# Three of the norm's scales and shifts as TensorE's sums, 36 matmuls ahead of them, the row of c loaded behind x

## The chip, the cores and the metric

One core of one Trainium2 chip runs the whole program in one launch. The time is device microseconds of that core, the median of several runs; lower is better. TensorE (PE) does matmuls, VectorE (DVE) and ScalarE (ACT) the elementwise work; SyncE (SP) issues nearly all DMAs from one queue, in the order of its program.

## The reference, cut to what matters

The program is two blocks over x of 512 tokens by 1024 features. The first begins with an adaptive norm, whose scale and shift come from a row c:

```python
mod = jax.nn.silu(c) @ w_ada[layer] + b_ada[layer]
shift1, scale1, gate1, shift2, scale2, gate2 = [m[:, None, :] for m in jnp.split(mod, N_MOD, axis=-1)]
h = rms_norm(x, g_pre_mix[layer]) * (1.0 + scale1) + shift1
proj = h @ w_in[layer]          # [512, 1024] @ [1024, 3584]
```

Behind it come a convolution and a retention mixer, an MLP of 4096, a pooling mixer and a recurrent mixer with 16 heads, each between large projections. All is float32.

## The kernel before, in words

**The data.** Weights come in units of 128 partitions by 1024 float32 (512 KB). `unit_list()` (line 32) gives their order: matmul units (True) and units of w_ada (False). SyncE loads them in this order (`load`, line 403), each into a slot: a ring of 5 slots of RAW, and six units (5 to 10) into free rows of Z. A unit loaded into a used slot first waits for what emptied it, and everything behind it in the queue waits too. The order at the start is, with u for one unit: w_in 0, ada 0, ada 1, w_in 1, ada 2, ada 3, ada 4, ada 5, w_in 2, ada 6, ada 7, ada 8, ada 9, w_in 3, ada 10 to ada 15, w_in 4 and so on. These are units 0 to 19; unit 18 (ada 14) takes the slot of unit 13 (w_in 3) and unit 19 (ada 15) that of unit 14 (ada 10).

**A matmul unit** is split into a high part (WH, ScalarE, line 1671) and a low part (WL, VectorE, line 967), both in the fp32r format; the normed tokens are split likewise into HH and HL. Each product is three matmuls (`three`, lines 488 to 490): high by high, high by low, low by high.

**The norm's scale and shift.** For f from 0 to 7, ada 2f holds the weights of the scale of features 128f to 128f+127, one feature on each partition, and ada 2f+1 those of their shift. `first_modulation` (line 931) multiplies a unit by CB, which is silu(c) on every partition (line 1142), and sums along the row, on VectorE (line 937). ScalarE adds the biases (lines 1861 and 1865), applies scale and shift to the transposed tokens (line 1871) and rounds to HH (line 1874); VectorE makes HL (`first_low`, line 1155). VectorE's order for each f is: ada 2f, ada 2f+1, HL of f-1, and at f = 1, 3, 5 the low part of the next w_in unit.

**TensorE** transposes the normed tokens (`first_tokens`, line 631; the instruction's inputs are float32), and runs `group`, the first projection: for k from 0 to 7, 12 matmuls of 512 columns once HL of k is there. The column products that follow have all they need as soon as HH and HL are whole.

**Ahead of that** SyncE issues: vectors, constants, the row of c broadcast to 128 partitions (line 413), four tiles of x (line 415), the units. VectorE and ScalarE make silu(c) as columns (COL) and as rows (CB), the squares of x (lines 1145, 1757), the root (lines 1035 to 1053) and the normed tokens (lines 1067 and 1761). ScalarE's line 1847 is the sigmoid of the row of c.

All orders are written out by hand, an instruction stream for each engine; the waits are on counts of semaphores. `taken` counts units that VectorE has finished with, `banks.made` tells that TensorE has filled a PSUM bank.

Of the kernel before, what the change touches and what calls it, by code (L numbers as in the profile page):

```python
# [10 lines left out]
ALU = mybir.AluOpType  # L11
# [20 lines left out]
def unit_list():  # L32

    out = []
    for f in range(8):
        if f in (0, 1, 3, 5):
            out.append(("w_in", (f + 1) // 2, True))
        out += [("ada", 2 * f, False), ("ada", 2 * f + 1, False)]
    ada = iter(range(16, 48))  # L40
    for n in range(4, 28):
        out.append(("w_in", n, True))
        if n >= 12:
            out += [("ada", next(ada), False) for _ in range(1 + n % 2)]
    for name, n in (("w_out", 8), ("w_fc1", 32), ("w_fc2", 32), ("pool_in", 40), ("pool_out", 16),
                    ("hgrn_in", 64), ("hgrn_out", 16)):
        for i in range(n):
            out.append((name, i, True))
            if name == "w_fc1" and 6 <= i < 14:
                out.append(("ada", next(ada), False))  # L50
    return out

UNITS = unit_list()
GEMM = [i for i, u in enumerate(UNITS) if u[2]]
LENGTH = {name: sum(u[0] == name and u[2] for u in UNITS) for name in dict.fromkeys(u[0] for u in UNITS)}

# [152 lines left out]
def build(nc, a):  # L210
    with ExitStack() as ctx:
# [64 lines left out]
        def flat(i):  # L276

            return Z[:, i:i + 2, :].rearrange("p a b -> p (a b)")
# [122 lines left out]
        def sync_program(e):  # L401
            def load(i):
                name, n, _ = UNITS[i]
                if RBEFORE[i] is not None:
                    e.wait_ge(taken.sem, taken.of(RBEFORE[i]))
                e.dma_start(raw(i), a[name][n]).then_inc(s_raw[RSLOT[i]], 16)

            def row(to, i):
                e.dma_start(to, a["rows"][i].partition_broadcast(128)).then_inc(s_row, 16)

            e.dma_start(VEC[:, :], a["vec"]).then_inc(s_vec, 16)
            e.dma_start(CST[:, :], a["cst"][:, 0:C_D]).then_inc(s_cst, 16)
            e.dma_start(flat(0), a["rows"][5].partition_broadcast(128)).then_inc(s_c, 16)
            for t in range(4):
                e.dma_start(X[:, t, :], a["x"][128 * t:128 * t + 128, :]).then_inc(s_x[t], 16)
            for i in range(20):
                load(i)
            e.dma_start(POSI, a["positions"].partition_broadcast(128)).then_inc(s_pos, 16)
            for i in range(20, 25):
                load(i)  # L420
            e.dma_start(MSK[:, :], a["msk"]).then_inc(s_msk, 16)
            e.dma_start(DMASK, a["cst"][:, C_D:C_N]).then_inc(s_d, 16)
            for i in range(25, len(UNITS)):
                load(i)

                if UNITS[i][0:2] == ("w_in", 10):
                    e.wait_ge(hlo.sem, hlo.of("in", 7))
                    row(flat(24), 0)
                    row(flat(2), 1)
                if UNITS[i][0:2] == ("w_fc1", 12):  # L430
                    e.wait_ge(tdone.sem, tdone.of("out", "x", 3))
                    row(flat(28), 2)
                    row(flat(30), 3)
                if UNITS[i][0:2] == ("pool_in", 12):
                    e.wait_ge(*banks.taken(("fc2", 3, 1)))
                    row(G[:, :], 4)
            for t in range(3):
                e.wait_ge(zdone.sem, zdone.of("final", t))
                e.dma_start(a["out"][128 * t:128 * t + 128, :], flat(2 * t)).then_inc(s_out, 16)
            for n in range(2):  # L440
                if n == 0:
                    e.wait_ge(zdone.sem, zdone.of("final", 3))
                else:
                    e.wait_ge(normed.sem, normed.of("final"))
                e.dma_start(a["out"][384:512, 512 * n:512 * n + 512], flat(6)[:, 512 * n:512 * n + 512]).then_inc(
                    s_out, 16)
            e.wait_ge(s_out, 16 * 5)

        def tensor_program(e):  # L450
# [176 lines left out]
            def first_tokens(f):  # L627
# [4 lines left out]
                                    IDN)  # L632
                m.then_inc(banks.full[b], banks.fill(("x", "t", f), b))

            e.wait_ge(own.sem, own.of("ones"))
            e.wait_ge(s_cst, 16)
            e.wait_ge(normed.sem, normed.of("x", 1))
            e.wait_ge(own.sem, own.of("normed", "x", 3))
            for f in range(4):
                first_tokens(f)  # L640
            for k, _ in enumerate(group([("v", j) for j in range(4)], [0, 1, 2, 3], True, "in")):
                if k < 4:
                    first_tokens(4 + k)
# [260 lines left out]
        def vector_program(e):  # L904
# [26 lines left out]
            def first_modulation(f):  # L931

                for j in (1, 0):
                    i = UNITS.index(("ada", 2 * f + 1 - j, False))
                    e.wait_ge(*landed(i))
                    c = 8 if j else 16
                    e.scalar_tensor_tensor(out=raw(i), in0=raw(i), scalar=1.0, in1=CB[:, :], op0=ALU.mult, op1=ALU.mult,  # L937
                                           accum_out=MOD[:, c + f:c + f + 1]).then_inc(taken.sem, taken(i))
# [169 lines left out]
            def boundary(stage, gain):  # L1108
# [13 lines left out]
                if stage != "pout":  # L1122
# [10 lines left out]
            e.memset(ONES[:, :], 1.0).then_inc(own.sem, own("ones"))  # L1133
            e.wait_ge(s_vec, 16)
            e.wait_ge(copied.sem, copied.of("silu"))
            e.tensor_tensor(COL[:, 0:8], COL[:, 8:16], VEC[:, V_C:V_C + 8], ALU.mult).then_inc(own.sem, own())
            e.scalar_tensor_tensor(out=GB, in0=VEC[:, V_BADA + 8:V_BADA + 16], scalar=1.0,
                                   in1=VEC[:, V_GPRE1:V_GPRE1 + 8], op0=ALU.add, op1=ALU.mult).then_inc(
                                       own.sem, own("gb"))
            e.wait_ge(s_c, 16)  # L1140
            e.wait_ge(copied.sem, copied.of("silu row"))
            e.tensor_tensor(CB[:, :], flat(2), flat(0), ALU.mult).then_inc(own.sem, own("cb"))
            for t in (1, 3):
                e.wait_ge(s_x[t], 16)
                e.scalar_tensor_tensor(out=flat(2 + 2 * t), in0=X[:, t, :], scalar=1.0 / 1024, in1=X[:, t, :],
# [3 lines left out]
            token_factors("x", 0, 4)  # L1149
            normed_tokens("x", 2)  # L1150
            normed_tokens("x", 3)

            def first_low(k):
                e.wait_ge(hhi.sem, hhi.of("in", k))
# [2 lines left out]

            p.next, p.hi, p.unit = 20, 4, 4
            lo_to(1)
            for f in range(8):  # L1160
                first_modulation(f)
                if f:
                    first_low(f - 1)
                if f in (1, 3, 5):
                    lo_to((f + 3) // 2)
# [492 lines left out]
        def scalar_program(e):  # L1658
# [101 lines left out]
            def normed_tokens(stage, t):  # L1760
                e.activation(normal(stage, t), X[:, t, :], ACT.Copy, scale=RT[:, t:t + 1]).then_inc(
                    normed.sem, normed(stage, t))
# [80 lines left out]

            e.wait_ge(s_vec, 16)
            e.activation(COL[:, 8:16], VEC[:, V_C:V_C + 8], ACT.Sigmoid).then_inc(copied.sem, copied("silu"))
            e.wait_ge(s_c, 16)
            e.activation(flat(2), flat(0), ACT.Sigmoid).then_inc(copied.sem, copied("silu row"))
            for t in (0, 2):
                e.wait_ge(s_x[t], 16)
                token_squares("x", t)  # L1850
            hi_to(1)
            e.wait_ge(own.sem, own.of("factors", "x", 0))
            normed_tokens("x", 0)
            normed_tokens("x", 1)
            e.wait_ge(own.sem, own.of("gb"))
            for f in range(8):
                b = 4 + f % 4
                if f in (1, 3, 5):
                    hi_to((f + 3) // 2)
                e.wait_ge(taken.sem, taken.of(UNITS.index(("ada", 2 * f, False))))  # L1860
                e.activation(GA[:, f:f + 1], MOD[:, 8 + f:9 + f], ACT.Identity,
                             scale=VEC[:, V_GPRE1 + f:V_GPRE1 + f + 1], bias=GB[:, f:f + 1]).then_inc(
                                 copied.sem, copied())
                e.wait_ge(taken.sem, taken.of(UNITS.index(("ada", 2 * f + 1, False))))
                e.activation(MOD[:, f:f + 1], MOD[:, 16 + f:17 + f], ACT.Identity,
                             bias=VEC[:, V_BADA + f:V_BADA + f + 1]).then_inc(copied.sem, copied())
                if f > 1:
                    e.wait_ge(hlo.sem, hlo.of("in", f - 2))
                e.wait_ge(*banks.made(("x", "t", f)))
                e.wait_ge(copied.sem, copied.n)  # L1870
                e.activation(TMP[:, 2 + f % 2, :], PS[b][:, :], ACT.Identity, scale=GA[:, f:f + 1],
                             bias=MOD[:, f:f + 1]).then_inc(banks.free[b], 1)
                e.wait_ge(*banks.taken(("x", "t", f)))
                e.activation(HH[:, f, :], TMP[:, 2 + f % 2, :], ACT.Copy).then_inc(hhi.sem, hhi("in", f))
# [425 lines left out]
```

## Time and profile before

| | us |
|---|---|
| median of 3 runs | 1482.09 (1479.09 to 1482.83) |
| the profiled execution | 1482.02 |
| its span | 1480.2 |
| PE busy in the span | 1445.2 (98%) |
| DVE busy | 871.0 (59%) |
| ACT busy | 563.5 (38%) |

The span is what the trace covers, from the first to the last instruction; 1.8 us of the execution's time lie outside it. PE's busy time is of pipelined matmuls with modelled ends, so the distance from one start to the next says more than the length of one. Every window of the trace begins at the span's start.

### The profile page before, as it was taken

Reading aid. Unit: us, or ns where it says so; the run is one execution under the profiler, and the core shown is the slowest. Engines: PE = TensorE matmul, PEld = TensorE weight load, DVE = VectorE, ACT = ScalarE, POOL = GpSimd, SP = SyncE. Lnnn points to the kernel's source line nnn. Section 1 sums busy time; section 2 is a strip of 40 time slices with the busy share of each in tenths; the row PEclk is TensorE's granted clock in tenths of the full one; section 3 lists DMA queues with packets and bytes.
Section 4 is the critical chain, followed back from the end, with each engine's and each line's share of the span. In section 5 each row is a group of like instructions: output and inputs, shape, how many; then the busy total and the mean of one; then the engine's idle time right before and its main releaser. Section 6 shows DMA issues by size and latency. Waiting matters only on the chain.

```text
span 1480.2 us, 18490 instructions
## 1 busy us (share of the span) xinstructions
PE 1445.2 (98%) x7204; PEld 1202.9 (81%) x7204; DVE 871.0 (59%) x1718; ACT 563.5 (38%) x1025; POOL 0.2 (0%) x4
## 2 busy tenths in 40 slices
PE   4999999999999999999999999999999999999998
PEld 3788788988888887988888888888888888888786
DVE  7876767543333335656457435325878777788545
ACT  5422345422232224533333334333444444444331
POOL 0000000000000000000000000000000000000000
PEclk9999999999999999999999999999999999999999
DMA  8645542353233334123233232232222222122221
GB/s 330 219 142 213 185 157 72 127 199 96 90 100 100 98 91 139 51 92 115 73 98 121 81 112 89 96 100 72 72 62 67 72 72 67 63 72 72 71 71 58
DMA packets 43863, 158.31 MB, mean 107 GB/s; under 512 B 4864, under 2 KB 5248, under 8 KB 43776
## 3 DMA queue, kind: packets, MB, share of 16 engines
q1 hardware_dynamic: 43776, 157.12, 32.4%
q8 instruction: 58, 0.95, 0.3%
q14 instruction: 29, 0.24, 0.1%
HBM read 155.00 MB, written 2.10 MB: 106 GB/s over the span
## 4 chain that ended last, share of the span: by engine, by line
PE 93%; DVE 4%; DMA 1%; ACT 1%; issue 1%; SPq 0%; ACTq 0%; DVEq 0%
PE PS L488 29%; PE PS L490 28%; PE PS L489 28%; PE PS L772 1%; PE PS L820 1%; PE PS L783 1%; PE PS L484 1%; PE PS L824 1%; PE PS L814 1%; PE PS L792 1%; PE PS L800 1%; DVE RAW L937 1%; DMA X<-in_x 1%; PE PS L839 1%; DVE WL L967 0%
## 5 line engine op out<-in xcount | busy, mean ns | idle before, releaser
L488 PE MATMUL PS<-HH,WH 128*128 128x512 f32 (+1 forms) x1088 | 432.2, 397 | 0.0
L490 PE MATMUL PS<-HH,WL 128*128 128x512 f32 (+1 forms) x1088 | 418.3, 384 | 0.0
L489 PE MATMUL PS<-HL,WH 128*128 128x512 f32 (+1 forms) x1088 | 417.2, 383 | 0.0
L967 DVE TENSOR_TENSOR WL<-RAW,WH 128x1024 fp32r<-128x1024 f32 x219 | 266.3, 1220 | 73.4 <-ACT WH L1671 73.1
L1671 ACT ACTIVATE WH<-RAW 128x1024 fp32r<-128x1024 f32 x219 | 230.8, 1057 | 185.5 <-PE PS L490 145.9
L490 PEld LDWEIGHTS PS<-HH,WL 128*128 128x128 f32 x1088 | 204.4, 188 | 42.0
L488 PEld LDWEIGHTS PS<-HH,WH 128*128 128x128 f32 x1088 | 204.8, 188 | 37.6 <-issue 1.0
L489 PEld LDWEIGHTS PS<-HL,WH 128*128 128x128 f32 x1088 | 205.0, 188 | 37.0 <-issue 1.0
L488 PE MATMUL PS<-WH,ZH 128*128 128x512 f32 x400 | 155.9, 390 | 0.0
L490 PE MATMUL PS<-WH,ZL 128*128 128x512 f32 x400 | 155.6, 389 | 0.0
L489 PE MATMUL PS<-WL,ZH 128*128 128x512 f32 x400 | 155.6, 389 | 0.0
L1014 DVE TENSOR_TENSOR ZL<-Z,ZH 128x512 fp32r<-128x512 f32 x52 | 35.6, 691 | 141.8 <-ACT ZH L1730 141.8
L1730 ACT ACTIVATE ZH<-Z 128x512 fp32r<-128x512 f32 x52 | 32.4, 632 | 156.9 <-PE PS L490 156.9
L488 PE MATMUL PS<-WH,HH 128*128 128x512 f32 x208 | 84.2, 405 | 4.8 <-DVE HL L1155 4.8
L489 PEld LDWEIGHTS PS<-WL,ZH 128*128 128x128 f32 x400 | 75.1, 188 | 15.6
L490 PEld LDWEIGHTS PS<-WH,ZL 128*128 128x128 f32 x400 | 75.1, 188 | 15.6
L488 PEld LDWEIGHTS PS<-WH,ZH 128*128 128x128 f32 x400 | 75.1, 188 | 15.4
L490 PE MATMUL PS<-WH,HL 128*128 128x512 f32 x208 | 82.4, 396 | 0.0
L489 PE MATMUL PS<-WL,HH 128*128 128x512 f32 x208 | 82.2, 395 | 0.0
L1316 DVE TENSOR_TENSOR Z<-TMP 128x512 f32<-128x512 f32 x32 | 22.0, 693 | 90.4 <-ACT TMP L1965 90.3
L1965 ACT ACTIVATE TMP<-PS 128x512 f32<-128x512 f32 x32 | 19.0, 598 | 109.9 <-PE PS L490 109.6
L488 PEld LDWEIGHTS PS<-WH,HH 128*128 128x128 f32 x208 | 39.9, 192 | 14.2 <-DVE RAW L937 2.9
(259 smaller groups left out, 1774.2 us busy)
## 6 DMA issues: line engine op xcount, KB each, us to landing
RAW<-in_w_fc SPq DMA_DIRECT2D x64, 512.0 KB, 3.5
RAW<-in_hgrn_in SPq DMA_DIRECT2D x64, 512.0 KB, 3.5
RAW<-in_ada SPq DMA_DIRECT2D x43, 512.0 KB, 4.6
RAW<-in_pool_in SPq DMA_DIRECT2D x40, 512.0 KB, 3.6
RAW<-in_w_in SPq DMA_DIRECT2D x27, 512.0 KB, 4.5
RAW<-in_pool_out SPq DMA_DIRECT2D x16, 512.0 KB, 3.6
RAW<-in_hgrn_out SPq DMA_DIRECT2D x16, 512.0 KB, 3.5
RAW<-in_w_out SPq DMA_DIRECT2D x8, 512.0 KB, 4.1
```

Of the source, the lines that this page charges most:

```text
L484: m = e.transpose(PS[b][:, c:c + 128], normal(stage, t)[:, 128 * f:128 * f + 128], IDN)
L488: e.matmul(out, wh, xh, start=first, stop=False)
L489: e.matmul(out, wh, xl, start=False, stop=False)
L490: return e.matmul(out, wl, xh, start=False, stop=last)
L772: m = e.matmul(PAIR[:, 256 * i:256 * i + 192], t.f[:, c], t.qp[:, i, :], start=True, stop=True)
L783: m = e.matmul(PS[b][:, 64 * i:64 * i + 64].rearrange("p (n l) -> p n l", l=16), t.k[:, c], halves(t.q[:, c], 16)[1], start=True, stop=True)
L967: e.tensor_tensor(lo, raw(i), hi.bitcast(F32), ALU.subtract).then_inc(taken.sem, taken(i))
L1014: e.tensor_tensor(lo, Z[:, k, :], hi.bitcast(F32), ALU.subtract).then_inc(zlo.sem, zlo(z))
L1316: e.tensor_tensor(Z[:, f, :], TMP[:, f % 2, :], TMP[:, f % 2, :], ALU.mult).then_inc(zdone.sem, zdone("fc1", f))
L1671: e.activation(place(s)[0], raw(i), ACT.Copy).then_inc(whi.sem, whi(s))
L1730: e.activation(z_place(z)[0], Z[:, k, :], ACT.Copy).then_inc(zhi.sem, zhi(z))
L1965: e.activation(TMP[:, f % 2, :], PS[b][:, :], ACT.Relu).then_inc(banks.free[b], 1)
```

## The change

The order of the units changes at the start (w_in 0 and w_in 1 behind the ada units of their f). Three ada units (0, 1 and 3: scale and shift of f = 0, shift of f = 1) are laid out by the host with the contraction on the partitions, and `first_sums` makes their sums on TensorE, eight matmuls of one column for each, with COL as the moving operand. Bank 0 holds those of f = 0, bank 1 that of f = 1; ScalarE reads them in PSUM. TensorE begins with 36 matmuls of ONES by ONES (float32, 128 columns), whose result nothing reads. The row of c is loaded behind the four tiles of x, its sigmoid comes behind ScalarE's squares, and CB behind VectorE's normed tokens. The high part of w_in 0 comes behind ScalarE's normed tokens.

```diff
     for f in range(8):
-        if f in (0, 1, 3, 5):
+        if f in (3, 5):
             out.append(("w_in", (f + 1) // 2, True))
         out += [("ada", 2 * f, False), ("ada", 2 * f + 1, False)]
+        if f < 2:
+            out.append(("w_in", f, True))
...
+SUMMED = {0: 0, 1: 0, 3: 1}
...
             def load(i):
                 name, n, _ = UNITS[i]
                 if RBEFORE[i] is not None:
-                    e.wait_ge(taken.sem, taken.of(RBEFORE[i]))
+                    was = UNITS[RBEFORE[i]]
+                    if was[0] == "ada" and was[1] in SUMMED:
+                        e.wait_ge(*banks.made(("mod", SUMMED[was[1]])))
+                    else:
+                        e.wait_ge(taken.sem, taken.of(RBEFORE[i]))
...
-            e.dma_start(flat(0), a["rows"][5].partition_broadcast(128)).then_inc(s_c, 16)
             for t in range(4):
                 e.dma_start(X[:, t, :], a["x"][128 * t:128 * t + 128, :]).then_inc(s_x[t], 16)
+            e.dma_start(flat(0), a["rows"][5].partition_broadcast(128)).then_inc(s_c, 16)
...
+            def first_sums(b):
+                claim(b)
+                n = [u for u in SUMMED if SUMMED[u] == b]
+                for c, u in enumerate(n):
+                    i = UNITS.index(("ada", u, False))
+                    e.wait_ge(*landed(i))
+                    for k in range(8):
+                        m = e.matmul(PS[b][:, c:c + 1], raw(i)[:, 128 * k:128 * k + 128], COL[:, k:k + 1],
+                                     start=k == 0, stop=k == 7)
+                m.then_inc(banks.full[b], banks.fill(("mod", b), b))
             e.wait_ge(own.sem, own.of("ones"))
+            for _ in range(36):
+                e.matmul(PS[2][:, 0:128], ONES[:, :], ONES[:, :], start=True, stop=True)
+            e.wait_ge(own.sem, own.of("silu"))
+            first_sums(0)
             e.wait_ge(s_cst, 16)
             e.wait_ge(normed.sem, normed.of("x", 1))
             e.wait_ge(own.sem, own.of("normed", "x", 3))
             for f in range(4):
                 first_tokens(f)
+            first_sums(1)
...
             def first_modulation(f):
                 for j in (1, 0):
+                    if 2 * f + 1 - j in SUMMED:
+                        continue
...
             e.scalar_tensor_tensor(out=GB, ...)
-            e.wait_ge(s_c, 16)
-            e.wait_ge(copied.sem, copied.of("silu row"))
-            e.tensor_tensor(CB[:, :], flat(2), flat(0), ALU.mult).then_inc(own.sem, own("cb"))
...
             normed_tokens("x", 3)
+            e.wait_ge(s_c, 16)
+            e.wait_ge(copied.sem, copied.of("silu row"))
+            e.tensor_tensor(CB[:, :], flat(2), flat(0), ALU.mult).then_inc(own.sem, own("cb"))
...
-            e.wait_ge(s_c, 16)
-            e.activation(flat(2), flat(0), ACT.Sigmoid).then_inc(copied.sem, copied("silu row"))
             for t in (0, 2):
                 e.wait_ge(s_x[t], 16)
                 token_squares("x", t)
-            hi_to(1)
+            e.wait_ge(s_c, 16)
+            e.activation(flat(2), flat(0), ACT.Sigmoid).then_inc(copied.sem, copied("silu row"))
             e.wait_ge(own.sem, own.of("factors", "x", 0))
             normed_tokens("x", 0)
             normed_tokens("x", 1)
+            hi_to(1)
...
-                e.wait_ge(taken.sem, taken.of(UNITS.index(("ada", 2 * f, False))))
-                e.activation(GA[:, f:f + 1], MOD[:, 8 + f:9 + f], ACT.Identity,
+                if f == 0:
+                    e.wait_ge(*banks.made(("mod", 0)))
+                else:
+                    e.wait_ge(taken.sem, taken.of(UNITS.index(("ada", 2 * f, False))))
+                e.activation(GA[:, f:f + 1], PS[0][:, 0:1] if f == 0 else MOD[:, 8 + f:9 + f], ACT.Identity,
...
+                shift = (PS[0][:, 1:2], PS[1][:, 0:1])[f] if f < 2 else MOD[:, 16 + f:17 + f]
+                if f < 2:
+                    e.wait_ge(*banks.made(("mod", f)))
+                else:
+                    e.wait_ge(taken.sem, taken.of(UNITS.index(("ada", 2 * f + 1, False))))
+                m = e.activation(MOD[:, f:f + 1], shift, ACT.Identity, bias=VEC[:, V_BADA + f:V_BADA + f + 1])
```

## Rows read from the trace of the kernel before

**Rows 1.** Busy time by window: stretch, length, engines, PEclk, DMA share, GB/s.
```profile
0.00:60.00 60.00, 37.30 (x155) 30.20 (x156) 44.61 (x79) 34.77 (x56) 0.20 (x4) 0.97 0.81 297
60.00:1480.00 1420.00, 1407.91 (x7050) 1172.65 (x7048) 826.37 (x1640) 528.68 (x970) 0.00 (x0) 1.00 0.31 99
```

**Rows 2.** The chain that ended last, 30 to 48 us: start, length, what.
```profile
37.11 1.14 DVE WL L967
...
38.65 6.08 DMA RAW<-in_ada
...
45.98 0.61 DVE HL L1155
```

**Rows 3.** Timeline of DVE: start, length, line, operation, count, idle before.
```profile
8.19 1.23 DVE L1142 TENSOR_TENSOR CB<-Z 128x1024 f32<-128x1024 f32 x1 [4.98 <-ACT Z L1847]
...
12.45 1.23 DVE L1145 SCALAR_TENSOR_TENSOR Z<-X 128x1024 f32<-128x1024 f32 x1 [1.43 <-DMA X<-in_x]
...
15.50 1.42 DVE L1067 TENSOR_SCALAR Z<-X,COL 128x1024 f32<-128x1024 f32 x2
16.83 1.22 DVE L967 TENSOR_TENSOR WL<-RAW,WH 128x1024 fp32r<-128x1024 f32 x1
17.96 1.22 DVE L937 SCALAR_TENSOR_TENSOR RAW<-RAW,CB 128x1024 f32<-128x1024 f32 x1
...
19.11 1.22 DVE L937 SCALAR_TENSOR_TENSOR RAW<-RAW,CB 128x1024 f32<-128x1024 f32 x1
...
26.61 0.69 DVE L1155 TENSOR_TENSOR HL<-TMP,HH 128x512 fp32r<-128x512 f32 x1
27.21 1.22 DVE L937 SCALAR_TENSOR_TENSOR Z<-Z,CB 128x1024 f32<-128x1024 f32 x1
...
44.75 1.23 DVE L937 SCALAR_TENSOR_TENSOR RAW<-RAW,CB 128x1024 f32<-128x1024 f32 x1 [1.12 <-DMA RAW<-in_ada]
```

**Rows 4.** Timeline of ACT.
```profile
13.73 1.06 ACT L1671 ACTIVATE WH<-RAW 128x1024 fp32r<-128x1024 f32 x1 [1.42 <-DMA RAW<-in_w_in]
15.50 2.19 ACT L1761 ACTIVATE Z<-X,COL 128x1024 f32<-128x1024 f32 x2 [0.71 <-DVE COL L1053]
...
20.37 0.29 ACT L1865 ACTIVATE MOD<-MOD,VEC 128x1 f32<-128x1 f32 x1 [0.70 <-DVE RAW L937]
20.76 0.78 ACT L1871 ACTIVATE TMP<-PS,MOD,COL 128x512 f32<-128x512 f32 x1
21.57 0.63 ACT L1874 ACTIVATE HH<-TMP 128x512 fp32r<-128x512 f32 x1
22.10 1.04 ACT L1671 ACTIVATE WH<-RAW 128x1024 fp32r<-128x1024 f32 x1
```

**Rows 5.** Timeline of PE, matmuls alone, 17 to 60 us.
```profile
17.94 3.65 PE L631 MATMUL PS<-CST,Z 128*128 128x128 f32 x16 [17.94 <-ACT Z L1761]
23.38 0.76 PE L488 MATMUL PS<-WH,HH 128*128 128x512 f32 x1 [1.79 <-DVE HL L1155]
...
26.85 0.40 PE L490 MATMUL PS<-WH,HL 128*128 128x512 f32 x1
...
27.78 0.60 PE L631 MATMUL PS<-CST,Z 128*128 128x128 f32 x4
28.14 0.48 PE L488 MATMUL PS<-WH,HH 128*128 128x512 f32 x1
...
46.73 0.47 PE L488 MATMUL PS<-WH,HH 128*128 128x512 f32 x1 [2.52 <-DVE HL L1155]
...
50.68 0.40 PE L489 MATMUL PS<-WL,HH 128*128 128x512 f32 x1
```

**Rows 6.** Timeline of PE, 119.8 to 121 us, float32 matmuls of the retention.
```profile
119.85 1.05 PE L660 MATMUL PS<-Z 128*128 128x128 f32 x8
120.66 0.48 PE L488 MATMUL PS<-HH,WH 128*128 128x512 f32 x1
```

**Rows 7.** Busy time by window, one that has DMA throughout.
```profile
24.00:27.00 3.00, 3.00 (x9) 2.38 (x8) 3.00 (x6) 1.77 (x4) 0.00 (x0) 1.00 1.02 407
```

More of the change, by code:

```diff
@@ L1135, in vector_program @@
             e.wait_ge(copied.sem, copied.of("silu"))
-            e.tensor_tensor(COL[:, 0:8], COL[:, 8:16], VEC[:, V_C:V_C + 8], ALU.mult).then_inc(own.sem, own())
+            e.tensor_tensor(COL[:, 0:8], COL[:, 8:16], VEC[:, V_C:V_C + 8], ALU.mult).then_inc(
+                own.sem, own("silu"))
             e.scalar_tensor_tensor(out=GB, in0=VEC[:, V_BADA + 8:V_BADA + 16], scalar=1.0,
@@ L1159, in vector_program @@
             lo_to(1)
+            e.wait_ge(own.sem, own.of("cb"))
             for f in range(8):
@@ L1859, in scalar_program @@
                     hi_to((f + 3) // 2)
-                e.wait_ge(taken.sem, taken.of(UNITS.index(("ada", 2 * f, False))))
-                e.activation(GA[:, f:f + 1], MOD[:, 8 + f:9 + f], ACT.Identity,
+                if f == 0:
[3 more added lines that the diff above has]
+                e.activation(GA[:, f:f + 1], PS[0][:, 0:1] if f == 0 else MOD[:, 8 + f:9 + f], ACT.Identity,
                              scale=VEC[:, V_GPRE1 + f:V_GPRE1 + f + 1], bias=GB[:, f:f + 1]).then_inc(
                                  copied.sem, copied())
-                e.wait_ge(taken.sem, taken.of(UNITS.index(("ada", 2 * f + 1, False))))
-                e.activation(MOD[:, f:f + 1], MOD[:, 16 + f:17 + f], ACT.Identity,
-                             bias=VEC[:, V_BADA + f:V_BADA + f + 1]).then_inc(copied.sem, copied())
+                shift = (PS[0][:, 1:2], PS[1][:, 0:1])[f] if f < 2 else MOD[:, 16 + f:17 + f]
[4 more added lines that the diff above has]
+                m = e.activation(MOD[:, f:f + 1], shift, ACT.Identity, bias=VEC[:, V_BADA + f:V_BADA + f + 1])
+                if f < 2:
+                    m.then_inc(banks.free[f], 1)
+                    e.wait_ge(*banks.taken(("mod", f)))
+                else:
+                    m.then_inc(copied.sem, copied())
                 if f > 1:
@@ L2266 @@
     features = ada.T.reshape(48, 128, 1024)
+    scale_shift = features[[8 * j + f for f in range(8) for j in (1, 0)]]
+    sums = columns(ada)[[8 * j + f for f in range(8) for j in (1, 0)]]
     arrays = {
@@ L2278 @@
         "msk": msk,
-        "ada": np.concatenate([features[[8 * j + f for f in range(8) for j in (1, 0)]], shares[16:24],
+        "ada": np.concatenate([np.stack([(sums if u in SUMMED else scale_shift)[u] for u in range(16)]), shares[16:24],
                                features[24:40], shares[40:48]]),
```

## The prediction

> **What bounds the kernel now.** I read the windows first. From 60 us to the end TensorE is busy for 1407.91 of 1420 us; before 60 us only for 37.30 of 60 [rows 1]. All edits lie in the first 45 us, so they can shift the start of TensorE's long stretch and little else. What is worth asking is when that stretch begins, and who sets it.
>
> The chain from 30 to 48 us answers [rows 2]. VectorE makes the low part of w_in 3, which ends at 38.25. That frees the slot for ada 14, and ada 15 is queued behind it; the DMA on the chain starts at 38.65 and lasts 6.08 us; VectorE sums ada 15 from 44.75 [rows 3]; HL of k = 6 starts at 45.98; TensorE takes k = 6 up at 46.73 after 2.52 us idle [rows 5]. Behind it nothing waits in this stage. So the end moves with the moment at which VectorE finishes w_in 3 (call it L3, 38.25), if the rest of the chain keeps its 8.48 us.
>
> TensorE's records also show two speeds: 0.43 us for 512 columns (1.2 GHz) from 23.38 to 26.85 and from about 47.3 to 50.68, 0.23 us (2.4 GHz) between and behind [rows 5]. The first slow stretch costs nothing, as the stage waits for VectorE anyway. The second costs some eight matmuls by 0.20 us = 1.6 us, and it followed the idle 2.52 us.
>
> **VectorE's side, taken away.** Three sums leave, at 1.15 us each by the distance of two starts, 17.96 and 19.11 [rows 3]: 3.45 us. CB (1.23) does not leave; it stood at 8.19, in time in which VectorE waited for x, and comes behind the normed tokens, where VectorE is busy: +1.2. The row of c goes behind x: it is 512 KB, at 407 GB/s [rows 7] 1.28 us, so the last tile of x is there 1.28 earlier and its squares start at 11.15 instead of 12.45; the root then ends 3.05 later at 14.2 (15.50 before) [rows 3]. Normed tokens (1.42 for two [rows 3]) to 15.6, CB to 16.8. The row itself lands at about 12.4, its sigmoid is done by 13.5, so CB waits for neither.
>
> The low part of w_in 0 needs its high part. ScalarE now makes its normed tokens first: 14.2 + 2.19 = 16.4, and the high part follows, 1.06, to 17.4 [rows 4]. The unit is third in the queue now: w_in 0 landed at 13.73 as the first [rows 4], the third place lands at 16.3. VectorE starts the low part at 17.45, against 16.83: 0.6 late. The saving of 1.28 is used up by CB and by this step. Low part to 18.6, ada 2 to 19.75 (landed 17.5).
>
> **TensorE's side, added.** The 36 matmuls of ONES write a bank that is not in use, from about 1.0. Nothing in the trace is such a matmul. The retention's float32 products are nearest: 8 records from 119.85 to 120.66 [rows 6], that are four matmuls, since each float32 product has two records: 0.20 us a matmul at 2.4 GHz. The slow end: transposes, with one record each, take 3.65/16 = 0.22 at the start and 0.09 (27.78 to 28.14 for four) later [rows 5]; two records at the slow pace are 0.43. Ends: 36 x 0.20 = 7.2 and 36 x 0.43 = 15.5. I take slow for some 4 us, as in both slow stretches, then fast: 9 x 0.43 + 27 x 0.20 = 9.3, to 10.4. TensorE is then idle until ada 0 lands (first place, 13.7), 3.3 us, more than the 2.52 that put it back. So I take the sums as beginning slow: 8 x 0.43 = 3.4 to 17.1, then 8 x 0.20 to 18.7. Bank 0 is seen at 18.9. The 16 transposes at 0.09 go to 20.2; ada 3 has landed at 18.8; eight more sums to 21.8. A sum of one column has no row either; below its price is that of a fast transpose (0.09), above it the slow 0.43; weight loads are as wide as in the retention, so I keep 0.20 fast.
>
> The Trainium skill bears on two of these choices. "TensorE: Matmul & The Clock Gate", HAM oscillation, says that waiting between bursts puts the clock back, and that each burst starts cold again; the trace agrees at 46.73, and by this rule the 36 matmuls buy nothing for the sums, as I have it. The same page, LDWEIGHTS, makes a weight load of 128 columns 128/1.2 = 107 ns at any clock; by that the sums would be 0.21 each even slow (an estimate), bank 0 would be full at 17.3, and the total would be that of the first rival.
>
> **ScalarE and the chain of k = 0 and 1.** Scale 0 from 19.0, shift 0, the application from 19.75, HH from 20.55 [rows 4], the high part of w_in 1 from 21.1 (22.10 - 21.57 behind HH). Shift 1 comes at 22.35, with bank 1 seen at 22.0; then 0.39 to the application (20.37 to 20.76), 0.81 to HH, 0.63 for it: 24.2. On VectorE, HL 0 ends at 21.8, the low part of w_in 1 waits to 22.2 and ends at 23.35, ada 4 and 5 at 25.65 (landed 21.4 and 22.7), HL 1 at 26.25 (0.60 as from 26.61 to 27.21 [rows 3]). HH 1 is not waited for, by 1.5 us.
>
> **From there to L3** the order is as before: six sums (ada 6 to 11) 6.9, three HL 1.8, two low parts 2.27, together 11.0. ada 6 and 7 land at 25.2 and 26.5 by 1.28 each, and ada 11 at 32.9; none is late in this line. L3 = 26.25 + 11.0 = 37.25. That is 1.0 us earlier than 38.25. Of 3.45 us taken away, 2.45 are lost to the later start, to HH 0, which now hangs on bank 0, and to w_in 1 behind it.
>
> **Waits added.** SyncE waits for bank 0 (18.9, before: 18.05) with units 11 to 15 behind it, and for bank 1 with unit 15. By the 1.28 us a unit, unit 11 has its place in the stream at 27.8 and unit 15 at 32.9; they go out 8.9 and 10.9 us ahead of that, more than the 6.08 of the DMA on the chain [rows 2], so the stream has no gap. ScalarE waits for bank 0 with everything behind it; that is in the sum. The host's new layout costs nothing on the device.
>
> **Sum.** The profiled execution has 1482.0; less 1.0 it is 1481.0. It stands 0.07 below the median of 1482.09, so the time is 1481.0. By my line TensorE waits before k = 6 as long as now, so the second slow stretch stays. What a measurement can't tell from no change is 0.3%, 4.4 us.
>
> **Rivals.**
> 1. The clock holds, or the sums cost 0.20 at any clock: bank 0 at 17.2, bank 1 at 20.2. Then ScalarE is early and only landings bound VectorE: ada 7 at 26.5, and from there ada 7 to 11, three HL and two low parts, 5 x 1.15 + 3 x 0.60 + 2 x 1.14 = 9.8; L3 = 36.3, 1.9 earlier: 1480.1. For it: float32 products are real matmuls, not transposes. Against: 3.3 us idle.
> 2. As the forecast or the first rival, and the wait before k = 6 falls so that the clock stays up: 1.6 more, 1478.5 to 1479.4. For it: TensorE may end k = 5 later than I think, and a shorter idle stretch may not put it back. Against: 2.52 us did, and nothing shortens the DMA in the chain.
> 3. Slower: TensorE at 1.2 GHz stands in the norm's path. ScalarE cannot apply f = 1 before bank 1, and HL 1 ends 2.6 us behind bank 1; VectorE is in order. Break-even is HL 1 at 38.25 - 11.0 = 27.25, bank 1 at 24.7. If the slow clock lasts from 13.7 through both rounds: 16 x 0.43 = 6.9 to 20.6, transposes 3.5 to 24.1, 3.4 to 27.5, HL 1 at 30.1, L3 at 41.1, +2.9: 1484.9. If even the 36 run slow, they end at 16.5, all is 2.8 later, +5.7: 1487.7. For it: the transposes at the start ran slow throughout [rows 5]. Against: both slow stretches ended after some 4 us.
> 4. No effect: ada 15's landing doesn't move with L3, as other DMAs fill the time: 1482.0. Against: the chain has the DMA issued right behind L3.
>
> **How the numbers follow.** Forecast 0.42, first rival 0.20, second 0.10, third 0.15 (a third of it in the upper case), fourth 0.13. The executions before spread by 3.7 us, so each case carries some 1.5 us to either side. The range is 1477.0 (second rival, less the spread) to 1485.5 (third rival's first case). Faster by over 0.3% needs below 1477.7: 0.07, second rival with the spread. Slower by over 0.3% needs above 1486.5: 0.06. Within: 0.87.
>
> **What would show it.** VectorE's low part of w_in 0 at 17.4, not 16.8; L3 at 37.2; ada 15 summed from 43.7; k = 6 at 45.7 with a slow stretch behind it; eight of the first 16 sums slow. Wrong if bank 1 is full after 24.7, if the 36 matmuls end after 13.7, if VectorE waits for a landing between ada 6 and w_in 3, or if TensorE from 60 us on is less busy than 1407.91 of 1420.

## The result, and the profile after

| | kernel before | changed kernel |
|---|---|---|
| median | 1481.63 us (1479.09 to 1483.60, 20 runs) | 1478.53 us (1476.67 to 1480.54, 20 runs) |
| ratio | | 0.9981, 95% interval 0.9974 to 0.9988 |
| the profiled execution, and its span | 1482.02, 1480.2 | 1478.98, 1476.9 |

The changed kernel is 2.8 us (by the ratio) to 3.1 us (by the medians) faster. Forecast were 1.0 us and 1481.0. The sign and the range hold, the size is short by two thirds.

By window, TensorE's time (stretch, length, PE, PEld, DVE, ACT, POOL, PEclk, DMA share, GB/s) in the changed kernel:

```profile
0.00:60.00 60.00, 57.31 (x290) 50.70 (x291) 43.03 (x75) 36.13 (x57) 0.20 (x4) 0.89 0.84 305
60.00:1476.00 1416.00, 1404.70 (x7036) 1169.94 (x7034) 824.58 (x1638) 527.16 (x968) 0.00 (x0) 1.00 0.30 99
```

Behind 60 us TensorE is idle for 11.3 us, nearly as before (12.1 [rows 1]). All that changed lies in the first 60 us. The change added 20 us of busy time there, nearly all of it dummy matmuls and sums; busy time is no measure of gain. What counts is the start of the first column product, as TensorE hardly waits behind it. From there to the end of the span it is 1426.3 us in both profiles.

Timeline of PE in the changed kernel: start, length, line (658: ONES; 651: the sums; 639: transposes; 496 to 498: `three`), operands, count, idle before:

```profile
1.04 10.62 PE L658 MATMUL PS<-ONES 128*128 128x128 f32 x72 [1.04 <-DVE ONES L1161]
13.31 4.37 PE L651 MATMUL PS<-COL,RAW 128*128 128x1 f32 x32 [1.65 <-DVE COL L1081]
17.54 3.65 PE L639 MATMUL PS<-CST,Z 128*128 128x128 f32 x16
20.99 3.41 PE L651 MATMUL PS<-COL,RAW 128*128 128x1 f32 x16
24.26 0.77 PE L496 MATMUL PS<-WH,HH 128*128 128x512 f32 x1
...
30.03 0.47 PE L496 MATMUL PS<-WH,HH 128*128 128x512 f32 x1
...
45.20 0.39 PE L496 MATMUL PS<-WH,HH 128*128 128x512 f32 x1
...
50.64 0.39 PE L496 MATMUL PS<-HH,WH 128*128 128x512 f32 x1
```

The value group starts at 24.26 (23.38 before [rows 5]), later and not earlier, and the column products at 50.64. In the trace of before that row stands at 53.89, which is 3.25 later. The 72 records of ONES are the 36 matmuls. After 13.31 no row has idle time in front of it, k = 6 (45.20) included; before, TensorE idled 2.52 us there [rows 5]. So in this profile it is no longer VectorE but TensorE's own stream that sets the end. The chain that ended last runs over TensorE alone from 13.31 on (start, length, what):

```profile
13.31 4.37 PE PS L651 x32
17.68 3.52 PE PS L639 x16
21.20 3.21 PE PS L651 x16
24.40 0.64 PE PS L496
```

Granted clock of the changed kernel (stretch, length, PE, PEclk, DMA share, GB/s):

```profile
14.00:16.00 2.00, 2.00 (x21) 1.00 1.03 422
16.00:18.00 2.00, 2.00 (x12) 0.54 1.04 420
24.00:26.00 2.00, 2.00 (x6) 0.50 1.03 410
28.00:30.00 2.00, 2.00 (x9) 0.55 1.03 410
```

It falls to half, 1.2 GHz, soon after 16 and comes back only at the end of k = 0, close to 30. There is no second slow stretch. This column can read 1.00 where the pace of the records says 1.2 GHz: in the kernel before it reads 1.00 from 24 to 27 us [rows 7], where the rows stand 0.43 us apart [rows 5].

Timeline of DVE in the changed kernel (965: sums, 995: low parts, 1184: HL):

```profile
26.20 0.69 DVE L1184 TENSOR_TENSOR HL<-TMP,HH 128x512 fp32r<-128x512 f32 x1 [1.55 <-ACT HH L1915]
...
36.63 1.22 DVE L995 TENSOR_TENSOR WL<-RAW,WH 128x1024 fp32r<-128x1024 f32 x1
37.76 1.22 DVE L965 SCALAR_TENSOR_TENSOR RAW<-RAW,CB 128x1024 f32<-128x1024 f32 x1
...
41.40 1.22 DVE L965 SCALAR_TENSOR_TENSOR RAW<-RAW,CB 128x1024 f32<-128x1024 f32 x1 [0.66 <-DMA RAW<-in_ada]
...
42.67 1.22 DVE L965 SCALAR_TENSOR_TENSOR RAW<-RAW,CB 128x1024 f32<-128x1024 f32 x1
```

Count L3 here as the start of the instruction behind the low part of w_in 3: 37.76, and 38.16 in the trace of before. The 3.25 us then split in three. L3 is 0.40 earlier. Ada 15 is summed from 42.67, 4.91 behind L3, where it was 44.75 - 38.16 = 6.59 [rows 3]: 1.68. From that sum to the first column product it is 7.97 against 9.14: 1.17. In the eight profiles below in which TensorE stays fast and VectorE sets k = 6 or nearly so (e1, e3, e5, e6, e8 to e11) this distance is 7.51 to 7.55, so the second slow stretch, which is missing, was worth 1.6, and 0.4 of it is lost as TensorE comes late to k = 6. Only the first part is what the change was said to do; the experiments are about the other two.

### The profile page after: what moved, and what is told of

It is laid out like the page before. It is cut to its first block, busy times and chain, and to the rows that moved or that the text cites. A ratio compares the mean times of both kernels' runs of the same rounds, so it can differ in the third digit from the quotient of the medians.

```text
span 1476.9 us, 18725 instructions
## 1 busy us (share of the span) xinstructions
PE 1462.0 (99%) x7324; PEld 1220.6 (83%) x7324; DVE 867.6 (59%) x1712; ACT 563.3 (38%) x1025; POOL 0.2 (0%) x4
## 4 chain that ended last, share of the span: by engine, by line
PE 95%; DVE 2%; ACT 1%; issue 1%; DMA 0%; SPq 0%; ACTq 0%; DVEq 0%
PE PS L496 29%; PE PS L498 28%; PE PS L497 28%; PE PS L798 1%; PE PS L846 1%; PE PS L809 1%; PE PS L492 1%; PE PS L850 1%; PE PS L840 1%; PE PS L818 1%; PE PS L826 1%; PE PS L865 1%; PE PS L651 1%; DMA X<-in_x 0%; PE PS L639 0%
## 5 line engine op out<-in xcount | busy, mean ns | idle before, releaser
L1503 DVE RECIPROCAL DG<-W 128x96 f32<-128x96 f32 (+1 forms) x64 | 49.7, 821 | 0.0
```

The source lines that it names most:

```text
L1503: e.reciprocal(i8[:, n, l], w8[:, n, l]).then_inc(own.sem, own("iw", h, i))
```

## The experiments

Each kernel was timed in 5 rounds beside the kernel before on the same chip (the last one has a single execution). The table gathers the profiles, one execution of each kernel, which can lie 1.1 us off the kernel's median (e2: 1481.8 and 1480.73, e9: 1478.09 and 1479.24); "packet" is the start of the 16 KB packet of the queue `q8 instruction` that lies nearest to L3.

| kernel | L3 | ada 15 summed, behind L3 | idle before k = 6 | slow stretch at k = 6 | first column product | packet | ratio (95%) |
|---|---|---|---|---|---|---|---|
| before | 38.16 | 6.59 | 2.52 | yes | 53.89 | 38.3 | |
| changed | 37.76 | 4.91 | none | no | 50.64 | 48.1 | 0.9981 (0.9974 to 0.9988) |
| e1_no_warm | 38.61 | 4.99 | 0.93 | no | 51.12 | 31.8 | 0.9992 (0.9983 to 1.0001) |
| e2_bridge | 36.36 | 6.91 | 2.85 | yes | 53.68 | 36.4 | 1.0000 (0.9992 to 1.0009) |
| e3_fill_k6 | 37.31 | 7.30 | 0.69 | no | 52.12 | 37.4 | 1.0002 (0.9993 to 1.0010) |
| e4_row_moved | 37.18 | 6.84 | 2.79 | yes | 53.18 | 37.2 | 1.0001 (0.9993 to 1.0010) |
| e5_positions_later | 37.19 | 6.76 | 2.33 | no | 51.49 | 37.3 | 1.0003 (0.9994 to 1.0011) |
| e6_two_sums | 36.13 | 5.01 | 0.94 | no | 48.67 | 47.7 | 0.9973 (0.9963 to 0.9984) |
| e7_bridge_fill | 38.00 | 7.07 | none | no | 53.75 | 38.0 | 1.0000 (0.9991 to 1.0009) |
| e8_after_again | 36.36 | 5.07 | 1.01 | no | 48.98 | 44.3 | 0.9976 (0.9966 to 0.9986) |
| e9_ones_only | 37.62 | 4.86 | 0.24 | no | 49.99 | 26.5 | 0.9984 (0.9975 to 0.9993) |
| e10_two_sums_order | 36.86 | 4.04 | none | no | 48.44 | 46.3 | 0.9971 (0.9960 to 0.9981) |
| e11_order_only | 37.08 | 4.32 | 0.26 | no | 48.95 | 40.6 | 0.9971 (0.9960 to 0.9982) |
| e12_before_again | 37.34 | 7.24 | 3.18 | yes | 53.74 | 37.5 | |

**e1_no_warm**: the changed kernel without the 36 matmuls.

```diff
-            for _ in range(36):
-                e.matmul(PS[2][:, 0:128], ONES[:, :], ONES[:, :], start=True, stop=True)
```

> The changed kernel without the 36 matmuls of ONES. Theory T (in the changed kernel TensorE itself sets the end of the value group: it starts the group at 24.26 us and is never idle after that): the 16 sums of f = 0 run at the slow pace of the later ones (0.204 us a record and not 0.132), bank 0 is full 2.3 us later, and so is the start of the group; the first column product starts at 52.9 instead of 50.64, the time is 2.3 us above the changed kernel. Rival V (VectorE and the landing of ada 15 set the end, as the prediction had it): VectorE's low part of w_in 3 ends up to 2.3 later, TensorE idles before k = 6, second slow stretch back: 2.3 + 1.6 = 3.9 us later. Rival W (the 36 matmuls buy nothing): no change within 0.5 us.

Measured: 1479.05 against 1480.73. The 32 records of the first sums take 6.96 us and not 4.37, as expected, but the 16 transposes behind them take 3.65 us, as in the changed kernel, and the pace comes back during the last sums (2.20 us for 16 records, not 3.41), so the first column product is hardly later: 51.12, not 52.9. By the ratios, which come from different chips, 1.6 us of the change's 2.8 are lost without the 36. None of the three theories gives this number, but the intervals of the two ratios overlap, so the times alone rule out neither T nor W.

**e2_bridge**: 45 matmuls and not 36.

```diff
-            for _ in range(36):
+            for _ in range(45):
```

> The changed kernel with 45 matmuls of ONES and not 36, so that TensorE has work until ada 0 lands (about 13.3 us) and the idle 1.65 us before the sums are gone. If the idle stretch is what took the clock down at 16.4: the sums, the transposes and the first k run fast, the value group starts at about 20.5 (HL of k = 0), then waits for VectorE at several k; theory T then expects an end bounded by HL of k = 6 at about 44 and k = 6, 7 at 5.5 us fast: first column product at 49.2 to 49.6, 1.0 to 1.4 us less time; with a second slow stretch 50.8, no gain. If it was not the idle stretch but the sums of one column and the transposes, which do not hold the clock: it falls by 20 us all the same, the group starts 0.5 to 2 earlier and still slow, first column product 0 to 1.3 earlier.

Measured: 1480.73, the same as before the change. Nine matmuls more give the whole gain back, which neither expectation has. TensorE's front is faster than in the changed kernel and L3 is early, but ada 15 is 6.91 behind it, TensorE idles before k = 6 and runs slow behind that.

```profile
14.02 3.90 PE L651 MATMUL PS<-COL,RAW 128*128 128x1 f32 x32
...
45.26 0.77 PE L496 MATMUL PS<-WH,HH 128*128 128x512 f32 x1 [2.85 <-DVE HL L1184]
...
53.68 0.39 PE L496 MATMUL PS<-HH,WH 128*128 128x512 f32 x1
```

These are rows of its PE timeline. As to the clock: no idle time stands before the sums, and it falls all the same.

```profile
16.00:18.00 2.00, 2.00 (x16) 0.81 0.99 397
18.00:20.00 2.00, 2.00 (x11) 0.50 1.05 420
20.00:22.00 2.00, 2.00 (x18) 0.84 1.01 404
```

So the fall does not need the idle 1.65 us. It came while sums of one column and transposes ran, but that these are the cause is not shown: the clock also came back while they ran (20 to 22 us here), and in e6 it reads 1.00 until 18 us, through the sums and the first 16 transposes.

**e3_fill_k6**: the kernel before, with matmuls in the idle time.

```diff
+                        if fresh and k == 6:
+                            claim(4)
+                            for _ in range(11):
+                                e.matmul(PS[4][:, 0:128], ONES[:, :], ONES[:, :], start=True, stop=True)
                         if fresh:
                             e.wait_ge(hlo.sem, hlo.of(fresh, k))
```

> The kernel before, and nothing of the change: ahead of the wait for HL of k = 6 TensorE runs 11 matmuls of ONES by ONES (float32, 128 columns) into bank 4, which is free there, about 2.2 us of work in the 2.5 us in which it was idle. If the idle stretch caused the second slow stretch (47.3 to 50.7): that stretch is gone, first column product at 52.3 instead of 53.9, 1.6 us less time. If it did not: the same time as the kernel before, or up to 0.3 more.

Measured: in the profile as expected, first column product at 52.12 and no slow stretch; in the timed runs nothing, 1480.62 against 1480.73. They would agree if the slow stretch were a matter of chance in the kernel before. e5 shows such a case: idle 2.33 and no slow stretch behind it. The mean granted clock of the single executions points the same way: it was 0.999 in the profiles of e3 and e5 and 0.998 in the three with the stretch and no matmul at the start (before, e4, e12). Of the 78 executions of the kernel before that were timed beside the experiments 21 had 0.999 and took 1480.1 us on average, the other 57 took 1481.4; e3 had 0.999 in 7 of 11. That the stretch makes this difference is not shown, as these executions have no profile.

**e4_row_moved**: the moves of the row of c alone, in the kernel before.

```diff
-            e.dma_start(flat(0), a["rows"][5].partition_broadcast(128)).then_inc(s_c, 16)
             for t in range(4):
                 e.dma_start(X[:, t, :], a["x"][128 * t:128 * t + 128, :]).then_inc(s_x[t], 16)
+            e.dma_start(flat(0), a["rows"][5].partition_broadcast(128)).then_inc(s_c, 16)
...
-            e.wait_ge(s_c, 16)
-            e.wait_ge(copied.sem, copied.of("silu row"))
-            e.tensor_tensor(CB[:, :], flat(2), flat(0), ALU.mult).then_inc(own.sem, own("cb"))
...
             normed_tokens("x", 3)
+            e.wait_ge(s_c, 16)
+            e.wait_ge(copied.sem, copied.of("silu row"))
+            e.tensor_tensor(CB[:, :], flat(2), flat(0), ALU.mult).then_inc(own.sem, own("cb"))
```

> The kernel before with the moves alone: the row of c loaded behind x, its sigmoid behind ScalarE's squares, CB behind VectorE's normed tokens, the high part of w_in 0 behind ScalarE's normed tokens; all 16 sums stay on VectorE. Theory T: x's last tile is there 2 us earlier, but the low part of w_in 0 starts only 0.2 to 0.5 earlier (its high part waits for the normed tokens), VectorE then goes on as before: 0 to 0.5 us less time. Rival (the move of the row carries the gain, as it brought x forward by 2.2 us): 2 us less.

Measured: 1481.26 against 1480.73, no difference. The row's move alone buys nothing that can be measured: ahead of the low part of w_in 0 VectorE now has CB (1.22 us) and 0.62 us of waiting for the high part, and ada 15 lands as late as before.

**e5_positions_later**: one DMA moved, in the kernel before.

```diff
-            e.dma_start(POSI, a["positions"].partition_broadcast(128)).then_inc(s_pos, 16)
             for i in range(20, 25):
                 load(i)
+            e.dma_start(POSI, a["positions"].partition_broadcast(128)).then_inc(s_pos, 16)
```

> The kernel before with one DMA moved: the positions, broadcast to 128 partitions, are issued behind unit 24 and not between units 19 and 20. In four of six profiles the last ada unit landed 6.1 to 6.8 us behind L3, in two 4.5 or less, and the GB/s of that stretch fall to 180 to 300 at a full DMA share. Theory P (the small pieces of the positions slow ada 15's DMA when they overlap it): ada 15 lands 4.4 us behind its issue, k = 6 starts at 45 instead of 46.7, 1.5 to 1.7 us less time, and if TensorE's idle stretch shrinks under 1 us the second slow stretch goes too, 3 us less. Rival (w_in units or chance slow it): no change within 0.5 us.

Measured: 1481.34 against 1481.12, and ada 15 is 6.76 behind L3. The positions are not what slows it. (TensorE also idles 0.65 us at 57.7 in this profile, for a low part.)

**e6_two_sums**: the shift of f = 1 back on VectorE.

```diff
-SUMMED = {0: 0, 1: 0, 3: 1}
+SUMMED = {0: 0, 1: 0}
...
-            first_sums(1)
```

> The changed kernel with the sums of f = 0 alone on TensorE; the shift of f = 1 is VectorE's again. TensorE can start the value group at about 21.2 instead of 24.26; VectorE's chain is hardly longer, as it waited 1.55 us for HH of k = 1 in the changed kernel. Theory K (the changed kernel gains because TensorE, late and slow at k = 0, has no idle stretch before k = 6 and so no second slow stretch): TensorE idles 1.5 to 2.8 us before k = 6 again, the first column product starts at 51.7 to 53 and not 50.64, so 1 to 2.4 us more time than the changed kernel. Rival (each sum taken off the critical start is a gain): 0 to 3 us less than the changed kernel.

Measured: 1477.02 against 1481.12, 0.9973, at least as fast as the changed kernel on that chip (0.9976). That is the rival's side, and my theory K falls: TensorE starts its group at 20.58, idles only 0.94 before k = 6, as ada 15 is early, and stays fast. The gain does not need a late, slow TensorE. The third sum buys nothing that these runs can tell.

**e7_bridge_fill**: 45 matmuls, and 14 before k = 6.

> The changed kernel with 45 matmuls of ONES at the start (no idle stretch before the sums) and 14 more ahead of the wait for HL of k = 6, in bank 4. With the 45 alone VectorE's L3 was at 36.45 but TensorE idled 2.85 us before k = 6 and then ran 24 matmuls at the slow pace, and the first column product started at 53.68. Theory K: with the idle stretch filled, k = 6 and 7 run fast: 45.3 + 5.5 = 50.8 with the late landing of ada 15, 49.2 with the early one: 2.9 to 4.5 us less than with the 45 alone, 0 to 1.4 less than the changed kernel. Rival (the clock falls all the same, or the fillers delay k = 6): 53.7, no gain.

Measured: 1481.17 against 1481.12. No idle time, no slow stretch at k = 6 and still 53.75: here bank 1 was full only at 24.6, and ada 15 was late again. TensorE reached k = 6 at 45.13, and the 28 records held it until 48.17. HL of k = 6 began at 46.22, and TensorE follows such a start by 0.83 us (45.90 to 46.73 before), so some 1.1 us of the 14 matmuls were too many: the rival's side. What a fill of the right length brings with the late DMA this run does not show.

**e8_after_again**: the changed kernel.

> The changed kernel again, as a measure of how much one profile says: if its gain is lasting, the first column product starts at 50.6 to 51.5 again with no slow stretch before it and the ratio is 0.998; if the landing of ada 15 or the clock varies from one execution to the next, it starts up to 2 us later in this profile.

Measured: 1477.65 against 1481.12, 0.9976. Ada 15 is 5.07 behind L3 again, on another chip. So the landing belongs to the program. The first column product does not repeat so well: 48.98, where 50.6 to 51.5 was expected, as here the clock came back before the third sum and bank 1 was full at 22.8. With e1 and e6 that is four profiles under 5.1 and, before e9, six over 6.5, with nothing between.

The packet tells them apart. The DMA view's line for each queue (queue, kind: packets, MB, share of 16 engines), first of the kernel before from 38 to 40 us, then of e2_bridge from 36 to 38, then of the changed kernel from 36 to 41:

```profile
q1 hardware_dynamic: 33, 0.14, 38.7%
q8 instruction: 1, 0.02, 3.0%
```

```profile
q1 hardware_dynamic: 20, 0.08, 31.9%
q8 instruction: 1, 0.02, 4.0%
```

```profile
q1 hardware_dynamic: 258, 0.93, 57.2%
```

In the changed kernel no such packet falls into this stretch, in which ada 14 and 15 are issued; the next is at 48.1. In the page of either kernel there are 58 of them:

```profile
q8 instruction: 58, 0.95, 0.3%
```

TensorE has 7204 matmuls and as many weight loads before, 248 to a packet, and with 45 matmuls at the start there are 59 packets. So I take the packets for TensorE's instructions, brought in as it goes along. The Trainium skill, "Runtime: NRT & Kernel Launch", Instruction fetch mechanics, says that an engine's instructions come in blocks of 16 KiB, 256 of them, by a DMA queue that the sequencer drives; the counts here agree. It also calls the cost of such a block mostly hidden. TensorE shows no wait for one here; what it does to the DMAs beside it the page does not say, and the next run tests it.

**e9_ones_only**: the kernel before with the 36 matmuls at the start, nothing else.

```diff
             e.wait_ge(own.sem, own.of("ones"))
+            for _ in range(36):
+                e.matmul(PS[2][:, 0:128], ONES[:, :], ONES[:, :], start=True, stop=True)
```

> The kernel before with the 36 matmuls of ONES at the start of TensorE's program and nothing else. The profiles so far fall into two kinds: where a 16 KB packet of the instruction queue (q8) falls between 36.4 and 38.3 us, just around the issue of ada 14 and 15 (the kernel before, 45 matmuls with and without the fillers, the filler alone, the row alone, the positions alone), ada 15 lands 6 us or more behind its issue; where it falls elsewhere (the changed kernel twice, without the 36, with two sums) 4.9 or less. Theory Q (that packet is TensorE's own instructions, every so many of them, and where it falls sets the landing): the 36 matmuls move it to about 22 us, ada 15 lands 4.4 to 4.9 us behind its issue, L3 stays, the first column product starts about 2 us earlier, up to 3.6 if the second slow stretch goes with the shorter idle time: 2 to 3.6 us less than before. Theory K (clock and sums alone carry the gain): TensorE has nothing to do from 11 to 17 us and the clock falls again: no change.

Measured: 1479.24 against 1481.62, 0.9984 (0.9975 to 0.9993). 36 matmuls whose result nobody reads, ahead of an idle stretch of 5.96 us, bring 2.4 us, where the whole change brings 2.8 and, in e8, 3.6; the intervals overlap, so what the rest of the change adds is not told from nothing. The packet fell into 26 to 28 us (predicted about 22). The chain of this kernel, and below it that of the kernel before on the same chip (start, length, what):

```profile
37.73 3.48 DMA RAW<-in_ada
...
42.48 1.23 DVE RAW L939 x2
43.71 0.61 DVE HL L1157
...
44.46 0.47 PE PS L488
44.93 0.23 PE PS L489
```

```profile
36.28 1.14 DVE WL L967
37.42 0.40 DVE RAW L937
37.81 6.74 DMA RAW<-in_ada
...
44.58 1.23 DVE RAW L937 x2
...
46.56 0.53 PE PS L488
47.09 0.43 PE PS L489
```

L3 is at 37.62 and 37.34. The chain runs over ada 14 in the one, 3.48 us, as ada 15 is already there when VectorE comes to it, and over ada 15 in the other, 6.74 us. TensorE's clock at the start cannot be the cause: with the 36 it was at half when the group started (0.50 from 22 to 28 us), and the gain came all the same. The clock has its part behind the landing: with 0.24 us idle before k = 6 there is no slow stretch (7.51 from ada 15's sum to the first column product, 9.16 in e12).

Part of the delay stands in SyncE's own rows, the issues of ada 14 and 15 (start, length; first e9, then e12):

```profile
37.73 0.80 SPq L406 DMA_DIRECT2D RAW<-in_ada  x2
```

```profile
37.44 1.41 SPq L406 DMA_DIRECT2D RAW<-in_ada  x2
```

Taken alone, the issue of ada 15 takes 0.43 us in all five profiles in which it lands early and 0.83 to 1.34 in all seven in which it lands late. So 0.4 to 0.9 of the some 2 us pass while SyncE issues the load, beside the packet, and the rest passes behind that.

**e10_two_sums_order** and **e11_order_only**: w_in 3 behind ada 10 and 11, once on top of e6, once in the kernel before. Ada 14 and 15 then wait for ada 10 and 11 and no more for L3.

```diff
-        if f in (0, 1, 3, 5):
+        if f in (0, 1, 3):
             out.append(("w_in", (f + 1) // 2, True))
         out += [("ada", 2 * f, False), ("ada", 2 * f + 1, False)]
+        if f == 5:
+            out.append(("w_in", 3, True))
```

> The changed kernel with the two sums of f = 0 alone, and w_in 3 behind ada 10 and 11 in the order of the units, so that ada 14 and 15 take the slots of ada 10 and 11 and wait for those alone. The chain from L3 over the DMA to ada 15 is cut: VectorE never waits for ada 14 or 15 and HL of k = 6 is made about 0.9 us earlier than with two sums alone (5 us behind L3, 3 sums and 2 HL): 0.7 to 1 us less than with two sums, 3.5 to 5 less than before. If w_in 4, which now waits for w_in 3, comes late, that is lost again.

> The kernel before with w_in 3 behind ada 10 and 11 in the order of the units, and nothing else. It takes the wait for ada 14 and 15 off the chain without moving any instruction of TensorE: if the landing of ada 15 is what the kernel before loses its time to, HL of k = 6 is ready at 43.5 to 44 instead of 46.6, TensorE has no idle stretch over 0.5 us there, and the time falls by 2.5 to 4 us with the 16 KB packet where it was. If TensorE were the limit already, the time falls by less than 1.

Measured: 1476.52 and 1477.17 against 1481.62, both 0.9971. Three lines in the order of the loads, without a sum on TensorE, bring 4.3 us, by the ratio more than the whole change (the intervals just overlap; against e8's, 0.9966 to 0.9986, they overlap widely); what else of the change is in e10 adds nothing measurable to them. VectorE's row of ada 15 in e11:

```profile
41.40 1.23 DVE L939 SCALAR_TENSOR_TENSOR RAW<-RAW,CB 128x1024 f32<-128x1024 f32 x1 [0.19 <-DMA RAW<-in_ada]
```

It still lands late, 5.92 us behind its issue, but was issued at 35.45: 0.19 us of waiting are left. The packet is at 40.6, while ada 15 is under way, and not "where it was", though none of TensorE's instructions was added or removed.

**e12_before_again**: the kernel before, a second profile.

> The kernel before again, one look on this chip: L3, the landing of ada 15, the idle stretch before k = 6 and the 16 KB packet. If the landing belongs to the program and not to the one execution: ada 15 lands 6 us or more behind its issue again, with the packet at 37 to 38.5.

Measured: 7.24 behind L3, idle 3.18, packet at 37.5, first column product at 53.74. The kernel before repeats itself.

## Why the prediction was right, and where it was short

**Who sets the end.** Right for the kernel before: all of the gain lies before 60 us, L3 and the chain behind it decide, and cutting that chain alone (e11) is worth 4.3 us. In the profile of the changed kernel TensorE sets the end itself (no idle time from 13.31 on), which the forecast, with a wait before k = 6 "as long as now", did not have; in e8 it waits again, 1.01 us.

**The front of VectorE.** The last tile of x came 2.19 us earlier, not 1.28 (squares at 10.26; 12.45 before [rows 3]), and CB was moved for 1.2 as costed. The low part of w_in 0 began at 16.84, against 16.83 [rows 3], where I had 17.45. HL 1 to L3 took 10.95 us; 11.0 was forecast.

**The sums on TensorE.** The ends bracketed them, the course was the wrong way round. The 36 ended at 11.66, not 10.4. The first sums ran fast (in e6, at full clock throughout, 3.57 us for 16, 0.22 a sum, against 0.20; at half clock they cost 0.41, so the first rival's "0.20 at any clock" does not hold), and the clock fell under them after 16; the transposes, the third sum and k = 0 were slow, where I had them fast. I held idle time for the cause; e2 has none and falls too. Bank 1 was full at 24.4, with break-even at 24.7: ScalarE waited 3.05 us for it and VectorE 1.55 for HH. That is the third rival's mechanism, only not far enough to put L3 behind that of before. e7 went further (24.6), e8 less (22.8, L3 36.36).

**L3.** Forecast 1.0 earlier; 0.40 in the profile, and 0.83 from e5 to e8 on one chip. About right, but two profiles of one kernel differ by as much (before: 38.16 and 37.34; changed: 37.76 and 36.36).

**The step that failed** is the condition in the first part: "if the rest of the chain keeps its 8.48 us". From the chain's L3 to k = 6 it did not keep it: ada 15 landed 1.68 us nearer to L3, and with it went the idle stretch and the slow one behind it, 1.17 net. The cause is none that the text weighed. The 36 matmuls, costed as 9.3 us of harmless work, moved the packets of TensorE's instructions, and one of these had lain on the issue of ada 14 and 15. e9 shows it: the matmuls alone move the packet, the landing and the time. The second rival had the number, 1478.5, by a mechanism that came true in e9 and the changed kernel (a shorter idle stretch), but it denied what caused it: "nothing shortens the DMA in the chain". That the time came out lower at all is so in part luck: with the packet at L3 (e2, e7) the same sums on TensorE brought nothing that can be measured.

Nor was it tried what the change is worth with the packet held in one place; e2 and e7, with the packet at L3, say that it is then worth nothing that can be measured, though with nine matmuls more.

## What to carry to other kernels

When a small edit to one engine's stream moves the time of a DMA that it has nothing to do with, look at where that engine's instruction packets fall: adding or removing instructions can shift them, and a gain that rests on this is lost with the next edit (45 matmuls for 36). Look first for what makes the wait itself: here a slot that was tied to the wrong unit, which three lines in the order of loads mend, for at least what the whole change brought. And a term taken over unchanged from the old chain deserves a range like any other.

## What the runs showed of the hardware

A 16 KB instruction packet beside the issue of a 512 KB load went with a landing some 2 us later (ada 15 used 6.6 to 7.3 us behind L3 in seven profiles, 4.9 to 5.1 in the five without), and with a longer issue on SyncE (0.83 to 1.34 us, 0.43 without).

TensorE's granted clock fell while it ran float32 matmuls of one column and transposes without a gap (e2: 1.00 until 16, 0.50 from 18 to 20), and in e6 it held through the same work (1.00 until 18). e2 and e7 have the same program up to k = 6 and differ in where the clock comes back (20 to 22 us in e2, past 28 in e7), so a single profile tells little of it. An idle stretch of 2.5 to 3.2 us before k = 6 was followed by the half clock in four profiles, one of 2.33 was not. A float32 sum of one column, with a weight load of 128 columns in each of its two records, took 0.22 us at 2.4 GHz (e6) and 0.41 at 1.2 (the changed kernel's third sum, 3.27 us for eight).
